# Mixture-of-experts block: an eleventh place for expert weights loaded twice more, the final norm's weight by a late transfer, expert 1's gather ahead of the last unit of expert 0

## The reference, cut to what matters

```
h = rmsnorm(x); proj = h @ w_in                      # attention, retention and gate columns
x = x + merged(attention, retention) @ w_out
hf = rmsnorm(x)
gates, experts = softmax(top4(hf @ w_router + b_router))     # 32 experts
for each expert e, on the tokens that chose it:
    gu  = hf @ w1[e] + b1[e]                         # w1[e]: 1024 x 2048, 8 MiB
    act = (clip(up) + 1) * min(gate, 7) * sigmoid(1.702 * gate)
    x  += gate_weight * (act @ w2[e] + b2[e])        # w2[e]: 1024 x 1024, 4 MiB
out = rmsnorm(x) * norm_final_g
```

## Time and profile before

| what | value |
|---|---|
| three timed executions | 1229.3, 1227.3, 1227.49 us; median 1227.49 |
| the profiled execution | 1227.92 us |
| its span, first to last instruction | 1225.9 us |
| granted TensorE clock | 0.999 |
| TensorE busy | 1169.0 us (95%) |
| VectorE, ScalarE, GpSimd busy | 428.0, 207.7, 58.5 us |
| moved by transfers | 461.79 MB, mean 377 GB/s |

### The profile page before, as it was taken

The page is one execution under the profiler, slowest core; times in us unless marked ns, Lnnn a source line. Parts: engine busy times, 40 slices in busy tenths (PEclk is TensorE's granted clock), DMA queues, the critical chain, the costliest instruction groups (busy, mean ns, idle before and its releaser), DMA issues.

```text
span 1225.9 us, 17199 instructions
## 1 busy us (share of the span) xinstructions
PE 1169.0 (95%) x7154; PEld 588.0 (48%) x7154; DVE 428.0 (35%) x741; ACT 207.7 (17%) x306; POOL 58.5 (5%) x43
## 2 busy tenths in 40 slices
PE   9999999999999999999999999999999899999897
PEld 8888888888643334333333333333333333333332
DVE  5886764655632223222222222222222222222222
ACT  6444553534400000000000000000000000000001
POOL 0850000000300000000000000000000000000000
PEclk9999999999999999999999999999999999999999
DMA  9756437877889999999999999999999999999996
GB/s 310 272 207 217 161 138 258 317 283 320 337 350 428 431 433 433 429 431 434 433 430 430 433 433 432 429 433 434 432 429 433 433 433 428 433 433 434 428 423 255
DMA packets 47522, 461.79 MB, mean 377 GB/s; under 512 B 4985, under 2 KB 6978, under 8 KB 32290
## 3 DMA queue, kind: packets, MB, share of 16 engines
q1 hardware_dynamic: 44760, 458.97, 89.9%
q10 hardware_dynamic: 2730, 2.36, 0.7%
HBM read 459.19 MB, written 1.07 MB: 375 GB/s over the span
## 4 chain that ended last, share of the span: by engine, by line
PE 66%; DMA 32%; DVE 1%; SPq 1%; ACT 0%; issue 0%; DVEq 0%; ACTq 0%
PE ps L1289 19%; DMA w_ring<-in_w 19%; PE ps L1355 12%; DMA A_QK<-in_w 6%; DMA xb_and_att<-in_w 6%; PE ps L1006 4%; PE ps L1444 4%; PE ps L1014 3%; PE ps L1012 3%; PE ps L1013 3%; PE ps L1263 2%; PE ps L1007 2%; PE ps L1026 1%; PE ps L1139 1%; PE ps L1141 1%; PE ps L1140 1%
## 5 line engine op out<-in xcount | busy, mean ns | idle before, releaser
L1289 PE MATMUL ps<-w_ring,A_W 128*64 128x512 f32 x1216 | 272.5, 596 | 28.9 <-DMA w_ring<-in_w 28.4
L1890 DVE TENSOR_SCALAR A_W<-ps 128x512 f32<-128x512 f32 x32 | 22.1, 692 | 478.2 <-PE ps L1289 478.2
L1289 PEld LDWEIGHTS ps<-w_ring,A_W 128*64 128x64 f32 x1216 | 84.8, 137 | 200.9 <-issue 160.2
L1355 PE MATMUL ps<-w_ring,A_W 128*64 128x512 f32 x608 | 137.9, 595 | 0.0
L1534 DVE TENSOR_TENSOR w_parts<-w_ring,w_parts 128x1024 fp32r<-128x1024 f32 x76 | 109.9, 1463 | 56.4 <-ACT w_parts L733 55.5
L1289 PE MATMUL ps<-A_QK,A_W 128*64 128x512 f32 x416 | 93.2, 595 | 9.3 <-DMA A_QK<-in_w 9.3
L918 ACT ACTIVATE A_W<-ps 128x512 f32<-128x512 f32 x31 | 18.5, 597 | 462.9 <-PE ps L1336 462.9
L1289 PE MATMUL ps<-xb_and_att,A_W 128*64 128x512 f32 x384 | 86.2, 596 | 9.4 <-DMA xb_and_att<-in_w 9.4
L733 ACT ACTIVATE w_parts<-w_ring 128x1024 fp32r<-128x1024 f32 x75 | 78.9, 1058 | 64.6 <-PE ps L1007 32.1
L914 ACT ACTIVATE A_W<-A_W 128x512 f32<-128x512 f32 x32 | 20.2, 631 | 359.8 <-DVE A_W L1890 359.8
L1006 PE MATMUL ps<-hT_both,w_parts 128*128 128x512 f32 x224 | 79.3, 399 | 0.0
(11 more groups left out here) (266 smaller groups left out, 1198.7 us busy)
## 6 DMA issues: line engine op xcount, KB each, us to landing
w_ring<-in_w SPq DMA_DIRECT2D x110, 2048.0 KB, 35.2
A_QK<-in_w SPq DMA_DIRECT2D x38, 2048.0 KB, 35.1
xb_and_att<-in_w SPq DMA_DIRECT2D x35, 2048.0 KB, 35.2
w_ring<-in_w_in SPq DMA_DIRECT2D x36, 1024.0 KB, 7.3
w_ring<-in_w SPq DMA_DIRECT2D x8, 1024.0 KB, 23.7
w_ring<-in_w_ret_branch SPq DMA_DIRECT2D x2, 2048.0 KB, 10.9
xb_and_att<-in_w SPq DMA_DIRECT2D x4, 1024.0 KB, 20.6
A_W<-in_w_out SPq DMA_DIRECT2D x1, 2560.0 KB, 13.0
```

The lines of the kernel that those rows point to most:

```text
L1289: mm = pe.matmul(o, XT[:, k, :], hidden_columns(tile[:, j, :], c), start=(k == 0), stop=(k == KC - 1))
L1355: mm = pe.matmul(ps[CAP * c:CAP * c + CAP, 3, :], lhs, w2_tile(flat)[:, q % W2_ROWS, c * HALF:(c + 1) * HALF], start=False, stop=(q == FQ ...
L1890: dve.tensor_scalar(gl, bank(0), LIMIT, None, ALU.min).then_inc(s.g, 1)
```

## The change

Four things:

1. **Units 14 and 24** (w2 of expert 1, first half; w1 of expert 4, third unit) leave the ring and are loaded into the first 4096 words of A_W, where unit 3 was. Unit 14 is loaded in two halves, the first when one row of unit 3 has been used, the second when unit 3 has. All later units move one place forward in the ring, after unit 24 two, and freed_at(n) says how far s_used must be. For units 15 to 33 that is one less than before; from the pair 34 and 35 on it is what it was.
2. **The final norm's weight** is no longer spread by TensorE and copied by ScalarE: SyncE reads it from memory to all 128 partitions with one transfer of 512 KB, behind the last weight transfer.
3. **Expert 1's gather** stands ahead of unit 3; the filling products and the waits on main.scales and s_res behind it are gone from TensorE. Expert 0's tokens lie in a place of their own (XT_first, in gl), its sums in banks 6 and 7. ScalarE copies the second half of the residual into banks 6 and 7 after VectorE has read those sums, between sigmoid(0) and the copy of expert 0's activation.
4. **The first five rounds of experts** are written out on TensorE, and its loop has five rounds instead of six.

```
+        XT_first = gl.rearrange("p (k s) -> p k s", k=KC)
+        FIRST_BANK = 6
+        ONE_SHOT = A_W[:, 0:UNIT_WORDS]
+        ONE_SHOT_UNITS = {14: 48, 24: 64}
+        UNIT_BASE = [16, 16, 16, 64]
+        def ring_order(n):
+            return n - (n > 14) - (n > 24)
+        def freed_at(n):
+            q = ring_order(n) - RING
+            return q + (q >= 14) + (q >= 23) + 1
...
-            return flat, s_pair[pair], 32 * (n // RING + (pair >= 2)) + (16, 32, 0, 0, 0)[pair]
+            if n in ONE_SHOT_UNITS:
+                return ONE_SHOT, s_unit[3], ONE_SHOT_UNITS[n]
+            q = ring_order(n)
+            pair, upper = q // 2 % (RING // 2), q % 2
...
-                for one in range(2):
-                    if n + one > RING + HALF_UNITS:
-                        sp.wait_ge(s_used, used + n + one - RING + 1)
+                for one in ((1, 0) if n in ONE_SHOT_UNITS else (0, 1)):
+                    if n + one in ONE_SHOT_UNITS:
+                        sp.wait_ge(s_used, 14 + 1)
+                        load_w1(sp, e, u + one, n + one)
+                    elif n + one > RING + HALF_UNITS:
+                        sp.wait_ge(s_used, freed_at(n + one))
...
+            sp.wait_ge(s_wu, OUT_DONE + W1_UNITS)
+            sp.dma_start(w2_tile(ONE_SHOT)[:, 0:2, :], w2_source(1, 0)[:, 0:2, :]).then_inc(s_unit[3], 16)
+            sp.wait_ge(s_used, W1_UNITS)
+            sp.dma_start(w2_tile(ONE_SHOT)[:, 2:4, :], w2_source(1, 0)[:, 2:4, :]).then_inc(s_unit[3], 16)
...
+            sp.wait_ge(s_lo, 2 * TT)
+            sp.dma_start(gain[:, :], bass.AP(g_final.tensor, 0, [[0, P], [1, D]])).then_inc(s_gain, 16)
...
+            pool.wait_ge(s_res, 2)
+            pool.memset(sc_w, 0.0).then_inc(main.swe, 1)
             pool.wait_ge(s_res, 2 * TT)
-            pool.memset(sc_w, 0.0).then_inc(main.swe, 1)
...
-            act.dma_start(g_rows[:, :], g_final.rearrange("(c p) -> c p", p=P)).then_inc(s_grows, 16)
...
-                    act.wait_ge(s_gainp, 1)
-                    act.wait_ge(s_lo, 2 * TT)
-                    act.activation(gain[:, :], bank(6, 2), ACT.Copy).then_inc(s_gain, 1)
-                    act.wait_ge(s_gain, 1)
...
+            act.wait_ge(s_res, 2)
             sigmoid(main, 0)
+            act.wait_ge(main.chain, 1)
+            store_residual(1)
+            act.wait_ge(s_res, 2 * TT)
             store_act(main, 0)
...
-                    hidden_unit(first_units[u], u, s_wu if u < HALF_UNITS else None).then_inc(s_used, 1)
+                    hidden_unit(first_units[u], u, s_wu, FIRST_BANK, XT_first).then_inc(s_used, 1)
                     if u == 2:
-                        hidden_bias(main, 0)
+                        hidden_bias(main, 0, FIRST_BANK)
                         second_scales()
-                        spread_gain()
+                        pe.wait_ge(s_lo, 2 * TT)
+                        gather(main, 1, scaled=True)
...
             hidden_first()
-            pe.wait_ge(s_lo, 2 * TT)
-            gather(main, 1, scaled=True)
-            pe.wait_ge(main.scales, 2)
-            fill(3, 8)
-            pe.wait_ge(s_res, 2 * TT)
-            with pe.Fori(0, (N_EXP - 2) // TURN) as r:
+            for k in range(TURN):
+                expert(k, k, 0)
+            with pe.Fori(1, (N_EXP - 2) // TURN) as r:
...
-            dve.wait_ge(s_res, 2 * TT)
+            dve.wait_ge(main.x, 1)
             store_scales(main, 1, scale_rows)
-            dve.wait_ge(s_used, W1_UNITS)
-            activate(main, 0, 1, scaled=True)
+            store_x(main, 1, scale_rows)
+            dve.wait_ge(s_used, W1_UNITS - 1)
             choose_bias(sel1, main.sel1, 1)
             slots(main, 2, 2)
+            dve.wait_ge(s_used, W1_UNITS)
+            activate(main, 0, b=FIRST_BANK)
+            dve.wait_ge(s_res, 2 * TT)
```

More of the change, by code:

```diff
@@ L381, in hybrid_block_kernel @@
         s_unit = [sem(f"w1_unit_of_first_or_last_or_extra_loaded{u}") for u in range(W1_UNITS)]
-        s_gainp = sem("final_gain_in_psum")
         s_used = sem("ring_units_used")
@@ L430, in place @@
         def place(n):
-            pair, upper = n // 2 % (RING // 2), n % 2
+            if n in ONE_SHOT_UNITS:
+                return ONE_SHOT, s_unit[3], ONE_SHOT_UNITS[n]
+            q = ring_order(n)
+            pair, upper = q // 2 % (RING // 2), q % 2
             flat = pairs[pair][:, upper * UNIT_WORDS:(upper + 1) * UNIT_WORDS]
-            return flat, s_pair[pair], 32 * (n // RING + (pair >= 2)) + (16, 32, 0, 0, 0)[pair]
+            return flat, s_pair[pair], 32 * (q // RING + (pair >= 2)) + (16, 32, 0, 0, 0)[pair]
         def load_w1(sp, e, u, n):
@@ L450, in load_expert_w1 @@
                 if n >= FIRST_PAIR:
-                    pair = n // 2 % (RING // 2)
+                    pair = ring_order(n) // 2 % (RING // 2)
                     to, source = pairs[pair].rearrange("p (j n) -> p j n", j=PAIR_ROWS), w1_both(e, u)
-                    sp.wait_ge(s_used, used + n + 1 - RING + 1)
+                    sp.wait_ge(s_used, used + freed_at(n + 1))
                     for odd in range(2):
@@ L471, in load_expert_w2 @@
             for u in range(W2_UNITS):
-                sp.wait_ge(s_used, used + n + u - RING + 1)
-                load_w2(sp, e, u, n + u)
+                if n + u not in ONE_SHOT_UNITS:
+                    sp.wait_ge(s_used, freed_at(n + u))
+                    load_w2(sp, e, u, n + u)
         def rows_of(view):
@@ L606, in _ @@
                 n = w1_number(N_EXP - 1, u)
-                sp.wait_ge(s_used, n - RING + 1)
+                sp.wait_ge(s_used, freed_at(n))
                 sp.dma_start(w1_tile(place(n)[0]), w1_source(N_EXP - 1, u)).then_inc(s_unit[u], 16)
             for n, (e, u) in enumerate(((N_EXP - 2, 0), (N_EXP - 2, 1), (N_EXP - 1, 0))):
-                sp.wait_ge(s_used, w2_number(e, u) - RING + 1)
+                sp.wait_ge(s_used, freed_at(w2_number(e, u)))
                 flat = place(w2_number(e, u))[0]
@@ L614, in _ @@
                     sp.dma_start(w2_tile(flat)[:, rows, :], w2_source(e, u)[:, rows, :]).then_inc(s_w2half[2 * n + h], 16)
-            sp.wait_ge(s_used, N_UNITS - 1 - RING + 1)
+            sp.wait_ge(s_used, freed_at(N_UNITS - 1))
             for j in range(W2_ROWS):
@@ L902, in _, with store_residual @@
                                accum_out=gden[:, t:t + 1]).then_inc(s_tke, 1)
-            for t in range(TT):
-                if t:
-                    act.wait_ge(s_gainp, 1)
-                    act.wait_ge(s_lo, 2 * TT)
-                    act.activation(gain[:, :], bank(6, 2), ACT.Copy).then_inc(s_gain, 1)
-                    act.wait_ge(s_gain, 1)
+            def store_residual(t):
                 for h in range(2):
@@ L911, in _ @@
                                    ACT.Copy).then_inc(s_res, 1)
+            store_residual(0)
             def sigmoid(s, i):
@@ L1281, in gather_first, with hidden_unit @@
                 mm.then_inc(main.gathered, 1)
-            def hidden_unit(flat, u, row_done=None):
+            def hidden_unit(flat, u, row_done=None, b=0, x=XT):
                 tile = w1_tile(flat)
@@ L1287, in hidden_unit @@
                     for c in range(4):
-                        o = ps[CAP * (c % 2):CAP * (c % 2) + CAP, c // 2, :]
-                        mm = pe.matmul(o, XT[:, k, :], hidden_columns(tile[:, j, :], c),
+                        o = ps[CAP * (c % 2):CAP * (c % 2) + CAP, b + c // 2, :]
+                        mm = pe.matmul(o, x[:, k, :], hidden_columns(tile[:, j, :], c),
                                        start=(k == 0), stop=(k == KC - 1))
@@ L1293, in hidden_unit, with hidden_bias @@
                 return mm
-            def hidden_bias(s, i):
+            def hidden_bias(s, i, b=0):
                 pe.wait_ge(s.sel1, i + 1)
                 for c in range(4):
-                    o = ps[CAP * (c % 2):CAP * (c % 2) + CAP, c // 2, :]
+                    o = ps[CAP * (c % 2):CAP * (c % 2) + CAP, b + c // 2, :]
                     pe.matmul(o, sel1[0:BIAS_ROWS, :], hidden_columns(bias[:, 0:2 * F], c), start=False, stop=False)
@@ L1327, in hidden_extra @@
                 for u in range(W1_UNITS):
-                    pe.wait_ge(s_unit[u], i * 16 + 48)
+                    pe.wait_ge(s_unit[u], i * 16 + UNIT_BASE[u] + 32)
                     hidden_unit(w1_part(u), u).then_inc(extra.w1_used, 1)
@@ L1378, in hidden_last @@
                 for u in range(W1_UNITS):
-                    pe.wait_ge(s_unit[u], 32)
+                    pe.wait_ge(s_unit[u], UNIT_BASE[u] + 16)
                     hidden_unit(place(w1_number(N_EXP - 1, u))[0], u).then_inc(s_used, 1)
@@ L1465, in second_scales @@
                 gather_scales().then_inc(main.gathered, 1)
[L1467 to L1473, removed]
             fill(0, 6)
@@ L1479, in _, with expert, transpose_previous @@
             hidden_first()
-            pe.wait_ge(s_lo, 2 * TT)
-            gather(main, 1, scaled=True)
```

(30 more changed lines are left out.)

## The result

The changed kernel takes **1231.62 us** (median of 8 executions, 1231.01 to 1232.45); the kernel before took 1227.45 beside it. The ratio is 1.0030 (95% interval 1.0019 to 1.0041): 4.2 us slower, where 1222.0 was forecast and faster had 0.83 of the chance. The profiled execution took 1231.96 us, with a span of 1229.9. In the experiments, one execution of pad58 took 1702.14 us at a granted clock of 0.655; it is left out of that kernel's median.

The account below looks back on a forecast made before the run. The expert stage was taken as bound by DMA bytes over rate: 5.8 us from closing the transfer hole less 0.3 for instruction fetch gives 5.5, so 1222.0 us; own range 1221.0 to 1223.3, 8 in 10 from 1220.7 to 1224.9.

Parts of the forecast that it names:

- What bounds the kernel: Expert stage: time is bytes over rate; only idle transfer time before the saturated stretch, a hole from 339.2 to 344.7, can be won.
- part 1: Units 14 and 24 outside the ring: unit 14 issued earlier closes the transfer hole, worth 5.8 us, bounds 4.9 to 6.4.
- part 3: TensorE between units 2 and 4: expert 1 starts 2.95 us earlier, near 336.5; worth nothing of its own at the end.
- the lead wasn't repaid: Rival at unit 34: a short queue there gives the lead back, leaving TensorE's 2.95 us, 1224.9 us; chance 0.10.
- The term of 5.8 us: Transfers in 334 to 364 us: rate rises from 347 to 430 GB/s over 30 us, a gain of 5.8 us.
- Part 2: Final norm's weight by one transfer last in the queue: 7.0 us of cover against 1.2 to 1.9, so no cost.
- The slower rival: At the final norm: weight read at one engine's pace lands at 1233.0, due 1220.5, giving 1234.5 us; chance 0.05.
- landed before 1210: Sign at the kernel's end that the forecast is right: the final norm's weight has landed before 1210 us.
- Part 4: Five experts written out on TensorE: one more instruction-fetch pass between 467 and 600 us, costing 0.3 us, bounds 0 and 0.4.
- the second pass of code: Instruction fetch for the written-out round, 467 to 600 us in the saturated stretch, priced at 0.3 us.
- TensorE's part: TensorE's earlier start on expert 1, 2.95 us, taken as all that remains if the lead is repaid at unit 34.
- the upper case: Gain from closing the hole counted by landings: 6.4 us; with no fetch cost 1221.1 us, chance 0.05.

Follow-up runs that it names:

- pad58: The changed kernel plus 58 filling products (116 instructions) ahead of expert 4's down units: 1222.94 us, ratio 0.9959 to the kernel before.
- pad58_again: The same kernel as pad58, run once more for a profile and a tighter time: 1223.10 us, ratio 0.9962 to the kernel before.
- pad58_stall: pad58 with GpSimd holding TensorE about 5.5 us at the start of each of five loop rounds: 1224.12 us, ratio 0.9970 to the kernel before.
- pad58_lane: pad58 plus 124 transfers of 4 KB to one partition each on ScalarE's queue, four per expert: 1238.34 us, ratio 1.0084 to the kernel before.

## Why the prediction was wrong

**What bounds the kernel**, **part 1** and **part 3** held in their mechanism. The halves of unit 14 went out at 334.38 and 336.10 (334.8 and 336.6 were forecast) and unit 15 at 339.53 (340.2). Expert 1 started at 335.88, 3.6 us earlier than before; 0.3 of that was there already at the first unit of expert 0. The transposes of expert 0 met no wait. Unit 34 was issued at 429.93 with 14.0 us to landing (430.6 and about 14), so the lead wasn't repaid. The term of 5.8 us stands by bytes: 2.34 MB more from 300 to 470 us, 5.4 us, and 2.46 MB in pad58_again, 5.7 us.

**Part 2** held: the weight landed at 1197.45 + 20.1 = 1217.6, wanted at 1223.37. The slower rival, its lateness, didn't come. My "landed before 1210" was off by the delay of the whole stream; in pad58_again, without the repeated fetch, it landed at 1189.66 + 20.2 = 1209.9.

**Part 4 is the step that failed.** It said "The written-out round brings one more such pass, between 467 and 600 us", priced at 0.3 us. I had seen that no packet passed on q8 in 470 to 604 us, concluded "the loop's body stays with the engine", and carried that over to a program in which 1677 instructions more stand ahead of the loop. The rows showed that the body stayed, not why. Against it I set the rule of the Trainium skill (Runtime: NRT & Kernel Launch, Instruction fetch mechanics) that a taken branch out of the current window forces a fetch and a stall, and used it only to spare the second pass. The useful sentence was the one beside it, on the size of TensorE's instruction memory, 128 KiB or 2048 instructions, and of its blocks. An estimate by it: 1738 instructions in 2048 leave so little room that the start counts. The runs agree with these sizes as far as they can: 67 packets with 0, 20 and 90 fillers, 31 with 58. They don't agree with the rule on branches: in the kernel before, TensorE branched back over the whole body five times without a packet on q8 from 470 to 1120 us.

The term should have read: four returns with about nine packets each, 36 more in all (67 against 31). The price of a packet was wrong too. By their bytes (0.59 MB at 430 GB/s) the 36 cost 1.4 us, by the 0.39 us for six of the earlier trace rows 2.3 us, and either would still have forecast a faster kernel. Measured, the repeated fetch costs 8.5 us (1231.62 - 1223.10), at most about 1.0 of it by TensorE's pauses, if they cost no more than pad58_stall's. That the rest, 7.5, goes with the packets is argued, by leaving the pauses out, and no run adds such packets alone. Two parts of it can be seen. From 600 to 1120 us q1 moves 223.29 MB where pad58_again's moves 224.50, 2.8 us at 430 GB/s; and the stream ends unevenly, 8 us at about half share, which is some 4 us of the slower engines' delay over the mean. pad58_lane shows that small traffic can do the second. That the fetch packets pass on about half of the engines is read from shares of 0.50 and 0.45 at that end; the rows don't name engines, and it stays open which they are and why each packet costs that much.

**The sum without the fetch.** pad58_again gives 1227.39 - 1223.10 = 4.3 us where 5.5 was forecast, inside the forecast's range by 0.2. Between the profiled executions it is 4.8 (1227.92 - 1223.10). The term that was mis-sized is the second pass of code: while it lasts, 470 to 600 us, q1 moves 55.87 MB where it moves 56.13 after it, 0.6 us by mean instead of 0.3; whether the slowest engine lost more no row shows. TensorE's part gave 2.1 with that pass in it, and the place 2.2 (2.65 and 2.9 by my terms); where the rest of the difference lies stays open. One bound doesn't follow from its terms either: 5.2 + 0.3 + 0.3 is 5.8, not the 6.4 from which the upper case and the low end of the range were taken.

**The chances.** None of my cases for slower had to do with code. 0.05 was too little for a change that moves every instruction behind it; a rival "the loop no longer stays" was missing, and the slower case that was worked out was a transfer that had 7 us of cover. Even with such a rival the prices at hand, 1.4 to 2.3 us, would have made the gain smaller and not a loss.

## What to carry to other kernels

With a long loop body (1738 instructions here), adding or removing a few dozen instructions ahead of it can change the time by more than the edit you are measuring: compare the packets of the instruction queue per round before and after, and try the same kernel with fillers before you judge a change. In a kernel bound by transfers, small transfers can cost far more than their bytes over all engines (15.2 us for 0.51 MB in pad58_lane). A mean share of 1.00 says nothing of how far the slowest engine is behind; look at how the share falls when the stream ends. And an idle time of the engine that isn't the bound can cost little, 1.0 us for 27.2 here, even when it is the most visible thing in the trace.

## What the runs showed of the hardware

- A loop of 1738 TensorE instructions was kept from round to round (31 instruction packets in the run) or fetched anew in each (67), depending on where it started; 58 filling products ahead of it moved the kernel from 1231.62 to 1223.10 us.
- Behind TensorE's pauses of 3.63, 3.26 and 2.56 us in the changed kernel the next sixteen fp32 products took 5.35 us, with a granted clock of 0.50 in 604 to 606 us; behind the one of 2.71 us they took 3.65 as usual.
- 124 transfers of 4 KB to single partitions, 0.51 MB, cost a stream of 459 MB 15.2 us; 31 transfers of 16 KB to 16 neighbouring partitions 7.1 us; to 16 partitions eight apart 2.1 us by ratios, 2.8 by medians.
